# A hybrid decoder block: attention logits from split fp32r operands, units half a slot later, five reorderings

## What is computed

```python
h = rmsnorm(x, norm1_w)
proj = h @ w_in                       # q,k,v,z,a,b of A; q, six k/v parts, gates of B; merge gates
y_a = gated_deltanet(...)
y_b = native_sparse_attention(...)
mixed = gate_a * (y_a @ w_proj_a) + gate_b * (y_b @ w_proj_b)
x = x + mixed @ w_out
h2 = rmsnorm(x, norm2_w)
x = x + (silu(h2 @ w_gate) * (h2 @ w_up)) @ w_down
```

```python
lc = einsum(qb, kc) * scale + bias            # compressed: 15 keys
ls = einsum(qb, k_sel) * scale + bias_s       # selected
lw = einsum(qb, kwin) * scale + head_bias(wd) # window
o = g0 * softmax(lc) @ vc + g1 * softmax(ls) @ v_sel + g2 * softmax(lw) @ vwin
```

## Time and profile before

| | |
|---|---|
| median of 3 runs | 557.66 us |
| the profiled execution | 559.03 us |
| its span | 557.2 us |
| TensorE busy | 547.5 us, 98% |
| VectorE busy | 396.8 us, 71% |
| ScalarE busy | 305.0 us, 55% |
| GpSimd busy | 69.7 us, 13% |
| chain that ended last | PE 85%, DVE 10%, ACT 2% |
| granted TensorE clock | full throughout |
| HBM read | 96.67 MB, 177 GB/s over the span |

### The profile page before, as it was taken

The page is one execution under the profiler, slowest core; times in us unless marked ns, Lnnn a source line. Parts: engine busy times, 40 slices in busy tenths (PEclk is TensorE's granted clock), DMA queues, the critical chain, the costliest instruction groups (busy, mean ns, idle before and its releaser), DMA issues.

```text
span 557.2 us, 9253 instructions
## 1 busy us (share of the span) xinstructions
PE 547.5 (98%) x3583; PEld 472.6 (85%) x3583; DVE 396.8 (71%) x649; ACT 305.0 (55%) x528; POOL 69.7 (13%) x107
## 2 busy tenths in 40 slices
PE   8999999999999999999999999999999999999996
PEld 8999999877777897788888888988888888888884
DVE  6879879976578737998886557567665766665763
ACT  6767669436445646656565343655545454545450
POOL 4221211683410000052000000000000000000000
PEclk9999999999999999999999999999999999999999
DMA  9945766455995352253544465755665766665622
GB/s 302 257 150 165 248 197 227 154 188 177 254 273 183 122 195 75 87 179 115 154 149 150 162 213 163 200 171 152 184 193 173 205 182 196 190 188 170 208 76 76
DMA packets 95467, 98.97 MB, mean 178 GB/s; under 512 B 5125, under 2 KB 75688, under 8 KB 95296
## 3 DMA queue, kind: packets, MB, share of 16 engines
q1 hardware_dynamic: 93168, 94.68, 55.1%
q0 software_dynamic: 1968, 2.64, 2.4%
q10 hardware_dynamic: 288, 1.05, 0.6%
HBM read 96.67 MB, written 1.84 MB: 177 GB/s over the span
## 4 chain that ended last, share of the span: by engine, by line
PE 85%; DVE 10%; ACT 2%; issue 2%; DMA 1%; DVEq 0%; ACTq 0%
PE ps L1596 17%; PE ps L1598 17%; PE ps L1597 17%; PE ps L1710 14%; PE ps L1713 7%; PE ps L1815 4%; DVE w_lo L1058 3%; PE ps L1601 3%; PE ps L1685 1%; PE ps L1975 1%; ACT w_hi L668 1%; DVE sc L1387 1%; DVE s_nm L1388 1%; PE ps L1950 1%; PE ps L1832 1%
## 5 line engine op out<-in xcount | busy, mean ns | idle before, releaser
L1058 DVE TENSOR_TENSOR w_lo<-raw,w_hi 128x2048 fp32r<-128x2048 f32 x74 | 170.6, 2306 | 99.0 <-ACT w_hi L668 98.9
L668 ACT ACTIVATE w_hi<-raw 128x2048 fp32r<-128x2048 f32 x74 | 141.5, 1913 | 73.5 <-PE ps L1598 64.9
L1710 PE MATMUL ps<-h_both,w_hi 128*128 128x512 f32 x352 | 122.7, 397 | 0.3 <-issue 0.2
L1713 PE MATMUL ps<-h_both,w_lo 128*128 128x256 f32 x352 | 91.2, 280 | 0.3 <-DVE h_both L1084 0.3
L1710 PEld LDWEIGHTS ps<-h_both,w_hi 128*128 128x128 f32 x352 | 63.8, 188 | 14.1 <-issue 1.5
L1713 PEld LDWEIGHTS ps<-h_both,w_lo 128*128 128x128 f32 x352 | 66.4, 189 | 4.0 <-issue 0.6
L1596 PE MATMUL ps<-w_hi,h_both 128*128 128x512 f32 x160 | 65.3, 408 | 0.1
L1598 PE MATMUL ps<-w_hi,h_both 128*128 128x512 f32 x160 | 62.6, 391 | 0.0
L1597 PE MATMUL ps<-w_lo,h_both 128*128 128x512 f32 x160 | 62.5, 391 | 0.0
L1596 PE MATMUL ps<-h_both,w_hi 128*128 128x256 f32 x208 | 59.5, 286 | 0.0
L1598 PE MATMUL ps<-h_both,w_lo 128*128 128x256 f32 x208 | 58.8, 283 | 0.0
(11 more groups left out here) (383 smaller groups left out, 950.2 us busy)
## 6 DMA issues: line engine op xcount, KB each, us to landing
raw<-in_w_in SPq DMA_DIRECT2D x29, 1024.0 KB, 5.2
raw<-in_w_gate SPq DMA_DIRECT2D x22, 512.0 KB, 4.0
raw<-in_w_up SPq DMA_DIRECT2D x22, 512.0 KB, 5.3
raw<-in_w_down SPq DMA_DIRECT2D x11, 1024.0 KB, 4.9
raw<-in_cmp_w SPq DMA_DIRECT2D x8, 1024.0 KB, 6.6
raw<-in_w_proj_a SPq DMA_DIRECT2D x4, 1024.0 KB, 5.1
raw<-in_w_proj_b SPq DMA_DIRECT2D x4, 1024.0 KB, 5.0
raw<-in_w_out SPq DMA_DIRECT2D x4, 1024.0 KB, 5.1
```

The source lines that it names most:

```text
L668: nc.scalar.activation(w_hi[s % NSPL][:], raw[RAW_OF[n]][:], ACT.Copy).then_inc(hi_done, 1)
L1058: nc.vector.tensor_tensor(w_lo[s % NSPL][:], raw[RAW_OF[n]][:], w_hi[s % NSPL][:].bitcast(f32), ALU.subtract).then_inc(lo_done, 1)
L1710: cross = lambda stop: pe.matmul(banks[part][:], hi[:, k, part * P:(part + 1) * P], h_both[:, :, k, :], start=(k == 0), stop=stop)
L1713: end = pe.matmul(banks[part][:, 0:SEQ], lo[:, k, part * P:(part + 1) * P], h_hi[:, k, :], start=False, stop=False)
```

## The change

It does these things:

1. Logits. ScalarE rounds the keys (both kinds, now one tensor `keysT`) and the queries to fp32r, `k_hi` and `q_hi`; VectorE subtracts to get `k_lo` and `q_lo`, in the places of the unrounded ones. 1,024 columns each time: keys and heads 0 to 3 in gz2's first half, before the burst, heads 4 to 7 in gz3's first half, after it. A unit's logits are now three fp32r matmuls over both kinds of keys at once (256 or 512 columns).
2. Units begin in gz3's first half in place of gz2's second, and end half a slot later, in mgb0.
3. The logits of unit i wait for `l_read` (L1387's result of unit i-1), no longer for its maximum.
4. ScalarE's step has the exponentials last, after `pt` and the output.
5. The split of nq0 stands on VectorE behind the gram stage, before it stood in front.
6. rn moves from cmpv1's slot to wv1's, behind Y5.
7. At gu0 `h_low` goes before the split of gu1.
8. x comes in four DMAs of 512 columns, with the squares summed in halves.

```diff
-FIRST_UNIT = 2 * AT["gz", 2] + 1
+FIRST_UNIT = 2 * AT["gz", 3]
...
+LOGIT_OPERANDS = {(AT["gz", 2], 0): 0, (AT["gz", 3], 0): 1}
...
-            for t in range(TT):
-                sp.dma_start(x_sb[:, t, :], x[0, t * P:(t + 1) * P, :]).then_inc(x_tile[t], 16)
+            for i in range(2 * TT):
+                t, c = i // 2, slice(i % 2 * 512, i % 2 * 512 + 512)
+                sp.dma_start(x_sb[:, t, c], x[0, t * P:(t + 1) * P, c]).then_inc(x_part[i], 16)
...
+            def logit_operands(p):
+                if p == 0:
+                    act.wait_ge(g_mm, stage_use("v1", NB - 1) + 1)
+                    act.wait_ge(m_out, TURN_KW + 1)
+                    nc.scalar.activation(k_hi[:], keysT[:], ACT.Copy).then_inc(k_hi_done, 1)
+                    act.wait_ge(nq_out, 4)
+                    nc.scalar.activation(q_hi[:, 0:4, :], nqT[:, 0:4, :], ACT.Copy).then_inc(q_hi_done, 1)
+                else:
+                    nc.scalar.activation(q_hi[:, 4 * p:4 * p + 4, :], nqT[:, 4 * p:4 * p + 4, :], ACT.Copy).then_inc(q_hi_done, 1)
...
             def unit(i):
-                if i < len(UNITS):
...
-                    act.wait_ge(s_done, i + 1)
...
                     nc.scalar.activation(nqT[:, h, t * P:(t + 1) * P], pv_ps[:, 0:P], ACT.Copy).then_inc(v_out, 1)
+                if i < len(UNITS):
...
+                    act.wait_ge(s_done, i + 1)
...
+            def logit_operands(p):
+                if p == 0:
+                    dve.wait_ge(k_hi_done, 1)
+                    dve.wait_ge(m_out, TURN_KW + 1)
+                    nc.vector.tensor_tensor(k_lo[:], keysT[:], k_hi[:].bitcast(f32), ALU.subtract).then_inc(k_lo_done, 1)
+                    dve.wait_ge(m_pe, LOGITS_C + 1)
+                    dve.wait_ge(nq_out, 4)
+                dve.wait_ge(q_hi_done, p + 1)
+                nc.vector.tensor_tensor(q_lo[:, 4 * p:4 * p + 4, :], nqT[:, 4 * p:4 * p + 4, :], q_hi[:, 4 * p:4 * p + 4, :].bitcast(f32),
+                                        ALU.subtract).then_inc(q_lo_done, 1)
...
-                    link(nc.vector.scalar_tensor_tensor(s, lg, col["rn"][:, h, t:t + 1], bg, ALU.mult, ALU.add))
+                    nc.vector.scalar_tensor_tensor(s, lg, col["rn"][:, h, t:t + 1], bg, ALU.mult, ALU.add).then_inc(l_read, 1)
+                    dve.wait_ge(l_read, i + 1)
...
+                    if n == AT["gu", 0]:
+                        h_low(KT, ROW_N2, (KT - 2, KT - 1))
                     if n + 1 < len(CHUNKS):
-                        for m in () if n in LATE_IN_SLOT else slot_splits(n):
+                        for m in () if n in LATE_IN_SLOT or n == AT["cmpk", 0] else slot_splits(n):
                             split_lo(m)
...
+                    if (n, half) == (AT["cmpk", 0], 1):
+                        split_lo(AHEAD[0])
...
-                        if n == AT["cmpv", 1]:
+                        if n == AT["wv", 1]:
...
-                        pe.wait_ge(s_done, i)
+                        pe.wait_ge(l_read, i)
...
-                    for a, keys in enumerate((ksT, kwT)):
-                        last = pe.matmul(log_ps[:, a * SEQ:a * SEQ + w], nqT[:, h, t * P:(t + 1) * P], keys[:, h // 4, 0:w], start=True, stop=True)
-                    last.then_inc(l_mm, 1)
+                    if h % 4 == 0 and t == 0:
+                        pe.wait_ge(q_lo_done, h // 4 + 1)
+                    three(((q_hi, q_lo), (k_hi, k_lo)), log_ps[:].rearrange("p (a c) -> p a c", a=2)[:, :, 0:w],
+                          lambda q: q[:, h, t * P:(t + 1) * P], lambda k: k[:, h // 4, :, 0:w], True, True).then_inc(l_mm, 1)
```

More of the change, by code:

```diff
@@ L290, in hybrid_block @@
         sub_tt = at("sub_tt", z_at + 7 * KB, [P, SUB * SUB])
-        nqT = own("nqT", [P, HEADS, SEQ])
+        nqT_at = take(8 * KB)
+        nqT, q_lo = at("nqT", nqT_at, [P, HEADS, SEQ]), at("q_lo", nqT_at, [P, HEADS, SEQ], f32r)
+        q_hi = ar(8, "q_hi", (P, HEADS, SEQ), f32r)
         bias_g = own("bias_g", [P, HEADS, SEQ])
-        ksT, kwT = own("ksT", [P, GROUPS, SEQ]), own("kwT", [P, GROUPS, SEQ])
+        keysT_at = take(4 * KB)
+        keysT, k_lo = at("keysT", keysT_at, [P, GROUPS, 2, SEQ]), at("k_lo", keysT_at, [P, GROUPS, 2, SEQ], f32r)
+        k_hi = ar(1, "k_hi", (P, GROUPS, 2, SEQ), f32r, off=2 * KB)
         vs, vw = own("vs", [P, TT, GROUPS, DH]), own("vw", [P, TT, GROUPS, DH])
@@ L361, in hybrid_block @@
         copied = sem("copied")
-        x_tile = [sem(f"x_tile{t}") for t in range(TT)]
+        x_part = [sem(f"x_part{i}") for i in range(2 * TT)]
         n1_in, bias_far, bias_set = sem("n1_in"), sem("bias_far"), sem("bias_set")
@@ L386, in hybrid_block @@
         cmp2_in = sem("cmp2_in")
+        k_hi_done, k_lo_done, q_hi_done, q_lo_done = (sem(n) for n in ("k_hi_done", "k_lo_done", "q_hi_done", "q_lo_done"))
         of_ready, zt, zs_done = sem("of_ready"), sem("zt"), sem("zs_done")
@@ L392, in hybrid_block @@
         hid_raw, hid_mm, hid_th, hid_done, pc_s, pc_e = (sem(n) for n in ("hid_raw", "hid_mm", "hid_th", "hid_done", "pc_s", "pc_e"))
[L393 to L394 removed]
+        l_mm, l_read, s_done, e_done, p_done, t_mm, t_out, v_mm, v_out = (sem(n) for n in (
+            "l_mm", "l_read", "s_done", "e_done", "p_done", "t_mm", "t_out", "v_mm", "v_out"))
         ya_hi_done, ya_lo_done, yb_hi_done, yb_lo_done = (sem(n) for n in ("ya_hi_done", "ya_lo_done", "yb_hi_done", "yb_lo_done"))
@@ L948, in unit @@
                     nc.scalar.activation(nqT[:, h, t * P:(t + 1) * P], pv_ps[:, 0:P], ACT.Copy).then_inc(v_out, 1)
+                if i < len(UNITS):
+                    h, t = UNITS[i]
+                    w = P * (t + 1)
+                    act.wait_ge(s_done, i + 1)
+                    for a in range(2):
+                        nc.scalar.activation(sc[i % 3][:, a, 0:w], sc[i % 3][:, a, 0:w], ACT.Exp,
+                                             bias=scol["nm"][:, 2 * (i % 3) + a:2 * (i % 3) + a + 1],
+                                             accum_out=scol["se"][:, 2 * (i % 3) + a:2 * (i % 3) + a + 1]).then_inc(e_done, 1)
             def second_norm(i):
@@ L1022, in _ @@
                         split_hi(n + 2)
+                    if (n, half) in LOGIT_OPERANDS:
+                        logit_operands(LOGIT_OPERANDS[n, half])
                     for i in slot_units(n, half):
@@ L1090, in _ @@
             nc.vector.memset(cin[1][:, :, 0:3], 0.0).then_inc(pre_dve, 1)
-            dve.wait_ge(x_tile[0], 16)
-            nc.vector.tensor_tensor_reduce(xn_sb[:, 0, :], x_sb[:, 0, :], x_sb[:, 0, :], 1.0, 0.0, ALU.mult, ALU.add,
-                                           accum_out=scol["c"][:, 1:2]).then_inc(xss, 1)
-            dve.wait_ge(xss, 1)
-            def mean_square(t):
-                nc.vector.tensor_scalar(scol["x"][:, t:t + 1], scol["c"][:, t + 1:t + 2], 64.0 / 9.0 / D_MODEL, 64.0 / 9.0 * EPS,
-                                        ALU.mult, ALU.add).then_inc(root_in, 1)
+            for i in range(2):
+                dve.wait_ge(x_part[i], 16)
+                c = slice(i * 512, i * 512 + 512)
+                link(nc.vector.tensor_tensor_reduce(xn_sb[:, 0, c], x_sb[:, 0, c], x_sb[:, 0, c], 1.0, 0.0, ALU.mult, ALU.add,
+                                                    accum_out=scol["c"][:, 1 + i:2 + i]))
+                if i == 0:
+                    link(nc.vector.tensor_scalar(scol["d"][:, 1:2], scol["c"][:, 1:2], 64.0 / 9.0 / D_MODEL, 64.0 / 9.0 * EPS, ALU.mult, ALU.add))
             def one_over_root(t):
@@ L1488, in _ @@
                         evacuate(n - 1, "b")
-                    if n == AT["gu", 0]:
-                        h_low(KT, ROW_N2, (KT - 2, KT - 1))
                     if CHUNKS[n - 1][0] == "wo" and n < AT["gu", 0]:
```

35 lines of the change are left out of this document (17 added, 18 removed).

## The result

The changed kernel takes 560.41 us (median of 4 runs, 559.49 to 561.51) beside 557.54 us for the kernel before (4 runs): a ratio of 1.0045, 95% interval 1.0031 to 1.0058. It is slower, by 2.9 us where no change (+0.2 us) was forecast, and outside the range that was given. Its profiled execution took 561.12 us.

The account below looks back on a forecast made before the run. TensorE, busy 547.5 of 557.2 us, was taken as the bound, with gaps where VectorE is behind. Terms -0.2 + 0.5 - 0.3 + 0.4 - 0.2 = +0.2 us gave a 557.9 us median, range 555.9 to 559.4.

Parts of the forecast that it names:

- units altogether: All 16 units: cheaper logits, two added waits and removed pt waits, -2.1 + 3.7 - 1.8 = -0.2 us.
- collision with GpSimd: Rival, chance 0.20: GpSimd's output multiplications delay VectorE at units 5 and 6 in mga2; two of 0.7 us, +1.4, 559.3 us.
- x in four pieces: At the start: half a tile's squares overlap the next half's landing, -0.2 us, between -0.5 and 0.
- Logits: In 16 units: three fp32r matmuls replace two fp32 ones, saving 0.18 us per wide unit and 0.09 per narrow, -2.1 us.
- New wait 1: Before unit 1's logits: TensorE waits 1.7 us for VectorE, whose third operand subtraction is not covered.
- new wait 2: Before mga0's second half: TensorE waits 2.0 us for zs, behind the sums of squares, in place of 0.39.
- Old waits removed: In the units: waits for pt go because ScalarE evacuates it before the exponentials, -1.8 us, between -1.3 and -2.4.
- nq0's split: Behind the gram stage: closes a 0.7 us gap at the fourth gram block, opens 1.3 before the fourth kq block, +0.5 us.
- rn: Ten operations moved behind Db and the transposes: Db's gap of 0.58 us closes, -0.3 us, between -0.6 and 0.
- h_low: At gu0: going first, it delays the split that gu1 waits for until 373.1, +0.4 us, between -0.5 and +0.5.
- the old wait: In the kernel before, in front of the chunk at 230.03: 0.39 us lost by TensorE.

Follow-up runs that it names:

- no_scale: The changed kernel with GpSimd's eight scalings of A's output on two columns each in place of 128: 558.76 us, ratio 0.999 to the kernel before.
- j_undone: The changed kernel with x in two DMAs and whole-tile squares again: 559.5 us, ratio 1.0022 to the kernel before.
- q1_late: The changed kernel with the operands of heads 4 to 7 made in mga2's second half: 560.58 us, ratio 1.005 to the kernel before.
- h_undone: The changed kernel with nq0's split in front of the gram stage again: 559.9 us, ratio 1.0048 to the kernel before.
- g_undone: The changed kernel with h_low behind gu1's split again: 561.05 us, ratio 1.006 to the kernel before.
- late_only: The kernel before with units half a slot later and nothing else: 560.86 us, ratio 1.0037 to the kernel before.
- early_operands: The changed kernel with units from gz2's second half again, operands moved to idle places, heads 4 to 7 in mga2's second half: 561.85 us, ratio 1.0078.
- best: As early_operands, with x in two DMAs and nq0's split in front of gram again: 560.65 us, ratio 1.0055 to the kernel before.
- sums_late: The changed kernel with the sums of squares behind zs on VectorE in place of in front: 561.32 us, ratio 1.0059 to the kernel before.
- both: The changed kernel with the edits of sums_late and q1_late together: 560.7 us, ratio 1.0048 to the kernel before.
- early_two: As best, with all operands made early and k_lo subtracted on GpSimd: 554.39 us, ratio 0.9926 to the kernel before.
- only_place: The changed kernel with units' start and operands as in early_two, x in four DMAs and nq0's split as changed: 556.15 us, ratio 0.9955.
- rest_only: The kernel before with only l_read, exponentials last, rn behind Y5 and h_low first: 555.73 us, ratio 0.9956 to the kernel before.
- x_four_only: The kernel before with x in four DMAs and squares in halves, nothing else: 559.5 us, ratio 1.0008 to the kernel before.

## Why the prediction was wrong

Two steps failed. The units altogether were to give 0.2 us and cost 2.6, because the working put down nothing for a collision with GpSimd and nothing for the clock. And x in four pieces was to give 0.2 us and cost 0.7 to 1.3, because the working left out the queue behind the DMAs.

By its terms, expected (in brackets) against measured:

- **Logits** (-2.1): right. Three wide ones start at 245.36, 245.59 and 245.81 and the next work at 246.05, 0.69 us; three narrow ones take 0.36. Against 0.87 and 0.44 (232.88 to 233.32) before that is 0.18 and 0.08 a unit, -2.1 in all.

```profile
245.36 0.39 PE L1636 MATMUL ps<-k_hi,q_hi 128*128 128x512 f32 x1
...
246.05 0.60 PE L1641 MATMUL ps<-ident,sc 128*128 128x128 f32 x4
```

- **New wait 1** (1.7) and **new wait 2** (2.0): right, 1.65 and 2.22.
- **Old waits removed** (-1.8): right in kind; by starts they were 2.1 over the whole stretch, since one of 0.24 before the transposes at 251.24 was not counted.
- **Units altogether** (-0.2): measured +2.6. The no_scale trace has -0.3: the step is right for what it holds. Two terms are missing. The **collision with GpSimd** (1.26 us at one product, unit 5's, where the rival had two of 0.7) was a rival at 0.20 and should have been in the sum: the working itself put VectorE a unit behind, which is the condition that the rival names. The Trainium skill (SBUF — State Buffer, Who interferes with whom) says that a VectorE instruction with two SBUF inputs contends with a GpSimd one that reads SBUF, and calls the shared ports an exclusive lock. The rows agree: GpSimd's multiplication ends at 255.26, and the product's own 0.69 us behind it would end at 255.95; it ended at 255.81. The **clock** was in no case at all: 1.6 us.
- **x in four pieces** (-0.2): wrong. The step looked at the squares and not at what is queued behind the DMAs. Two more issues hold SyncE for 1.2 us in front of ident and of the first weights: +1.3 in this trace, +0.7 in the mean.
- **nq0's split** (+0.5): right, +0.57 (110.95 and 1.05 make 112.0, where the working has 112.1). **rn** (-0.3): right, -0.25. **h_low** (+0.4): the wait at gu1 came as described, and up to there it costs 0.27. The working took 372.76 for the start of gu1, but that row holds two matmuls and gu1 begins with the second, at about 373.0; so its own 373.1 makes 0.1. Behind gu1 the changed kernel is 0.86 us shorter than before, of which the runs show no cause.

So the sum of +0.2 lacked 1.26 + 1.6 in the units and 0.9 to 1.5 at the start (0.7 or 1.3 where -0.2 stood), and had 1.0 too much behind the units (+0.4 where -0.6 was measured). The medians differ by less than the traces' last matmuls (2.9 against 3.6): the fall of the clock is not in every execution, and the start of the changed kernel's trace is 0.6 us later than the mean of its kind.

In six kernels with the changed kernel's second wait (changed, j_undone, q1_late, h_undone, g_undone, no_scale) the mean granted clock was 0.997 or less in 27 of 44 executions. With a second wait of 2.0 in late_only it was so in 5 of 12, and with the wait of 4.4 in early_operands and best in all ten. With the second wait at 1.1 (sums_late, both) it was so in 2 of 12. Without it, it was so in none of 19 (early_two, only_place, rest_only), in 1 of 12 in x_four_only and in 5 of 69 of the kernel before. The mean is a rough sign, for it doesn't say where the clock fell: the traces of early_two, only_place and rest_only have it low too, but only from 551 us on, behind the last matmul. What a fall costs is seen within one kernel: executions at 0.997 or less have a longer span than those at 0.999 or more, in the median by 1.5 us in j_undone, 1.8 in no_scale and 2.6 in late_only, part of which may be long ends. That the waits bring the clock down fits all of this; how much waiting it takes was not measured.

Why the change loses is the first result behind the list: of the two waits' 3.9 us late_only has 3.0 from the half slot alone. In the kernel before, a wide unit, its transposes and its values (2.06 us, 0.39 of them the old wait) covered `zs`; half a slot later only a narrow unit and two transposes do (0.6 us). The new subtraction of 1.22 us between `zs` and unit 0 accounts for most of the rest, at the first wait: moved away in q1_late it leaves 0.5 of the 1.65.

What stays open: why some executions need 1.4 to 2.2 us more behind the last matmul, and what h_low's edit does behind gu1.

## What to carry to other kernels

Added work goes where the busiest helper engine is idle in the trace, not beside the work that uses it: the same format put the last matmul 3.6 us later with the units and operands in one place, and 1.2 us sooner in another (3.0 with two edits undone), where one of the three subtractions also went to GpSimd. Before a start is shifted, list what used to run on the bound engine between a bank's last use and the next, since that is the cover of the evacuation. When your own working predicts waits of some microseconds on TensorE, add a term for the clock behind them, and when it puts an engine behind, price the meetings that this brings.
